# Retention loads issued by SP, the first pair's ahead of the stage; first keys turned on GpSimd; the rotation split around the head factor

## What is computed

```python
def retention_mixer(p, positions):
    q, k, v, g = _split(p, RET_SIZES)
    q = rotary(q, positions); k = rotary(k, positions) * (dk ** -0.5)
    def step(R, inp):                      # one chunk of 128 tokens
        s = einsum('bihd,bjhd->bhij', qc, kc) * decay_mask
        inner = einsum('bhij,bjhe->bihe', s, vc)
        cross = einsum('bihd,bhde->bihe', qc * q_decay, R)
        R = R * chunk_decay + einsum('bjhd,bjhe->bhde', kc * k_decay, vc)
        return R, inner + cross
    o = group_norm_heads(o, RET_GN_EPS)
    return silu(g) * o
merged = sigmoid(g_rw) * (y_rw @ w_branch_rw) + sigmoid(g_ret) * (y_ret @ w_branch_ret)
```

## Time and profile before

| what | value |
|---|---|
| median of three runs | 2634.45 us (2625.81 to 2635.38) |
| the profiled execution | 2635.51 us, its span 2633.5 us |
| PE busy over the span | 2428.1 us, 92% |
| DVE busy | 1237.1 us, 47% |
| ACT busy | 672.1 us, 26% |
| POOL busy | 752.0 us, 29% |
| chain that ended last, by engine | PE 77%, DVE 12%, DVEq 4%, ACT 3%, DMA 2% |

### The profile page before, as it was taken

How to read it: one execution, slowest core, us unless ns; L and a number is a source line. 1 busy time by engine, 2 the same in 40 slices (tenths; PEclk the granted TensorE clock), 3 DMA queues, 4 the chain that set the end, 5 groups by cost and what they waited for, 6 DMA issues and landing times.

```text
span 2633.5 us, 33584 instructions
## 1 busy us (share of the span) xinstructions
PE 2428.1 (92%) x12944; PEld 1961.6 (74%) x12944; DVE 1237.1 (47%) x1382; ACT 672.1 (26%) x1020; POOL 752.0 (29%) x386
## 2 busy tenths in 40 slices
PE   5899989999998996888998999999999986989896
PEld 4788878877886885777787788888777864767674
DVE  6644264335335442756556644444411417526623
ACT  3322222122222221333242211111223332023421
POOL 2311221131123110113464333333244434222132
PEclk9999999999999998999998999999999997999997
DMA  3211111121111115634443111111142220111011
GB/s 121 64 49 49 65 48 57 49 71 51 49 65 56 49 49 153 203 122 172 159 147 109 56 48 42 46 48 48 41 151 95 93 75 24 43 56 41 17 40 64
DMA packets 54872, 196.46 MB, mean 75 GB/s; under 512 B 5744, under 2 KB 7152, under 8 KB 53872
## 3 DMA queue, kind: packets, MB, share of 16 engines
q1 hardware_dynamic: 29952, 109.07, 12.6%
q10 hardware_dynamic: 24816, 85.84, 9.2%
HBM read 158.71 MB, written 36.18 MB: 74 GB/s over the span
## 4 chain that ended last, share of the span: by engine, by line
PE 77%; DVE 12%; DVEq 4%; ACT 3%; DMA 2%; issue 2%; ACTq 1%; POOL 0%; POOLq 0%; SPq 0%
PE psg L336 10%; PE psg L341 10%; PE psg L340 10%; PE psg L471 5%; PE psg L473 5%; PE psg L466 5%; PE psg L851 1%; PE psg L855 1%; PE psg L854 1%; PE psa L562 1%; PE psg L912 1%; PE psg L907 1%; PE psb L551 1%; PE psg L914 1%; PE psg L365 1%
## 5 line engine op out<-in xcount | busy, mean ns | idle before, releaser
L286 POOL CAST whi<-wraw 128x1024 fp32r<-128x1024 f32 (+1 forms) x164 | 186.9, 1139 | 1637.1 <-PE psg L466 612.3
L336 PE MATMUL psg<-xhi,whi 128*128 128x512 f32 x1152 | 459.7, 399 | 3.1 <-DVE pu L1461 2.7
L341 PE MATMUL psg<-xhi,wlo 128*128 128x512 f32 x1152 | 454.6, 395 | 0.0
L340 PE MATMUL psg<-xlo,whi 128*128 128x512 f32 x1152 | 452.9, 393 | 0.0
L288 POOL TENSOR_TENSOR wlo<-wraw,whi 128x1024 fp32r<-128x1024 f32 (+1 forms) x164 | 432.0, 2634 | 25.7 <-issue 6.3
L473 PE MATMUL psg<-xhi,wlo 128*128 128x512 f32 x640 | 260.8, 408 | 0.0
L466 PE MATMUL psg<-xhi,whi 128*128 128x512 f32 x640 | 260.0, 406 | 0.0
L471 PE MATMUL psg<-xlo,whi 128*128 128x512 f32 x640 | 259.9, 406 | 0.0
L336 PEld LDWEIGHTS psg<-xhi,whi 128*128 128x128 f32 x1152 | 216.3, 188 | 56.5 <-issue 5.1
L341 PEld LDWEIGHTS psg<-xhi,wlo 128*128 128x128 f32 x1152 | 216.2, 188 | 54.5
L340 PEld LDWEIGHTS psg<-xlo,whi 128*128 128x128 f32 x1152 | 216.2, 188 | 52.7 <-issue 1.0
(11 more groups left out here) (469 smaller groups left out, 4464.4 us busy)
## 6 DMA issues: line engine op xcount, KB each, us to landing
wraw<-w SPq DMA_DIRECT2D x208, 512.0 KB, 3.4
later_scratch<-stage ACTq DMA_DIRECT2D x40, 512.0 KB, 2.7
xres<-xt ACTq DMA_DIRECT2D x4, 1024.0 KB, 11.4
RV<-later_scratch ACTq DMA_DIRECT2D x4, 1024.0 KB, 12.2
RG<-later_scratch ACTq DMA_DIRECT2D x4, 1024.0 KB, 7.4
later_scratch<-rstage ACTq DMA_DIRECT2D x8, 512.0 KB, 2.7
mgr<-later_scratch ACTq DMA_DIRECT2D x8, 512.0 KB, 3.6
mgt<-later_scratch ACTq DMA_DIRECT2D x8, 512.0 KB, 4.6
```

The lines of the kernel that those rows point to most:

```text
L286: pool.tensor_copy(whi[:, u, 0:width], wraw[:, u, 0:width])
L336: mm = pe.matmul(psg[b][:, cols], whi[:, slot, w_cols], rhs_hi(k, cols), start=(k == 0), stop=False)
L340: pe.matmul(psg[b][:, cols], whi[:, slot, w_cols], rhs_lo(k, cols), start=False, stop=False)
L341: mm = pe.matmul(psg[b][:, cols], wlo[:, slot, w_cols], rhs_hi(k, cols), start=False, stop=(k == kts - 1))
```

## The change

- SP issues all retention loads, in between its weight blocks. The first pair's and the angles wait on tr_act 32 (ACT has copied the values of the last recurrent group), three of the RWKV results on gh_ready 16 in the same group. The fourth stays where it was made. The first pair gets tiles of its own (rraw_first, rswp_first, RTAB_first, RG0, RQD0, RKD0).
- The first pair's keys are turned and scaled by GpSimd, in four instructions behind the split of block 57 (B_BRW - 1). DVE turns only that pair's queries.
- For the other pairs `rotate` falls into two parts: the products stand where it stood, the sum and the keys' scaling between the two head factors.
- The first pair's second values go to psg[1] instead of psb, so that they need not wait for ACT's copy of the first.
- For p > 0 six of the branch matmuls move from behind the scores to ahead of the chunk sums.
- At the end the first two tiles of yret are split while the last head factor is under way, and PE does their product (12 matmuls) ahead of the last L410.

```diff
...
-        RV, RG = tiles("RV", 12, [P, 2, T]), tiles("RG", 14, [P, 2, T])
+        yrw = [tiles("yrw0", 9, [P, T]), tiles("yrw1", 2, [P, T]), tiles("yrw2", 3, [P, T]), YB]
+        RV, RG = tiles("RV", 12, [P, 2, T]), [spare("RG0", 0, [P, 2, T]), tiles("RG", 14, [P, 2, T])]
+        RQD = [tiles("RQD0", 6, [P, T]), tiles("RQD", 16, [P, T])]
+        RKD = [tiles("RKD0", 7, [P, T]), tiles("RKD", 17, [P, T])]
...
-        rraw = [spare("rraw0", 0, [P, 2, T]), tiles("rraw1", 18, [P, 2, T])]
-        rswp = spare("rswp", 2, [P, 2, T])
+        rraw = [tiles("rraw_first", 4, [P, 2, T]), tiles("rraw1", 18, [P, 2, T]), spare("rraw0", 0, [P, 2, T])]
+        rraw.append(rraw[1])
+        rswp = [tiles("rswp_first", 6, [P, 2, T]), spare("rswp", 2, [P, 2, T])]
...
+            def load_pair(p):
+                sp.dma_start(RTAB[p], ret_tab[p]).then_inc(sem("ret_in"), 16)
+                rows = later_d[6 * p:6 * p + 2]
+                sp.dma_start(rraw[p][:, :, :], rows.rearrange("a p t -> p a t")).then_inc(sem("ret_in"), 16)
+                for q in range(4):
+                    dst, src = q * 32, (q ^ 1) * 32
+                    sp.dma_start(rswp[1][dst:dst + 32, :, :], rows[:, src:src + 32, :].rearrange("a p t -> p a t")
+                                 ).then_inc(sem("ret_in"), 16)
+                load_values(p)
...
+            stream(0, B_BRW, 0)
+            for b in range(2):
+                sp.wait_ge(sem(f"stored{b}"), 80 + 16)
+            sp.wait_ge(sem("rot_stored"), 64)
+            sp.wait_ge(sem("tr_act"), 8 * PAIRS)
+            sp.dma_start(RTAB[0][:, :, :], ret_tab[0]).then_inc(sem("ret_in"), 16)
+            first_rows(1, sem("ret_in"))
+            for r in range(4):
+                sp.dma_start(rott[r * 32:r * 32 + 32, :, :], rot_d[:, 2 * (r % 2):2 * (r % 2) + 2, :]
+                             ).then_inc(sem("rot_in"), 16)
+            sp.dma_start(RC[:, :], mats[:, M_CENT_RET, :]).then_inc(sem("rv_in"), 16)
+            load_values(0)
+            first_rows(0, sem("rq_in"))
+            sp.wait_ge(sem("yrw_stored"), 16 * PAIRS)
+            sp.wait_ge(sem("gh_ready"), GROUPS * PAIRS)
+            for r in range(PAIRS - 1):
+                sp.dma_start(yrw[r][:, :], yrw_d[:, r, :]).then_inc(sem("yrw_in"), 16)
+            stream(B_BRW, B_BRW + 2, 0)
+            sp.wait_ge(g_full, T_BRW)
+            load_gates(0)
+            sp.wait_ge(sem("yrw_done"), PAIRS)
+            sp.wait_ge(sem("rv_tr"), 2)
+            for b in range(2):
+                sp.wait_ge(sem(f"stored{b}"), 80 * (PAIRS - 1) + 16)
+            load_pair(1)
+            for p in range(1, PAIRS):
+                stream(B_BRW + 2 * p, B_BRW + 2 * p + 2, 0)
+                sp.wait_ge(sem("rg_done"), p)
+                load_gates(p)
+                if p + 1 < PAIRS:
+                    sp.wait_ge(sem("rkd"), p + 1)
+                    sp.wait_ge(sem("rs_ready"), 2 * p)
+                    sp.wait_ge(sem("rv_tr"), 2 * p + 2)
+                    load_pair(p + 1)
+            stream(B_MRG, B_OUT + KT, 0)
...
             split_blocks(0, B_BRW)
+            pool.wait_ge(sem("ret_in"), 96)
+            pool.wait_ge(sem("rot_in"), 64)
+            key, other = rraw[0][:, 1, :], rswp[0][:, 1, :]
+            pool.tensor_tensor(key, key, rott[:, 1, :], ALU.mult)
+            pool.tensor_tensor(other, other, rott[:, 0, :], ALU.mult)
+            pool.drain()
+            pool.tensor_tensor(key, key, other, ALU.add)
+            pool.drain()
+            pool.tensor_tensor(RKD[0][:, :].rearrange("p (n c) -> p n c", c=P), key.rearrange("p (n c) -> p n c", c=P),
+                               RTAB[0][:, 3:4, :].broadcast_to([P, NB, P]), ALU.mult).then_inc(sem("rkd"), 1)
             split_blocks(B_BRW, B_MRG, PAIRS * P)
...
+                    if between and k == 2:
+                        between()
...
-                if h == 0:
+                dst = psb_t
+                if p == 0 and h == 1:
+                    pe.wait_ge(g_free[1], 8 * PAIRS + 2)
+                    dst = psc_t
+                elif h == 0:
...
-                pe.wait_ge(sem("rv_tm"), 2 * p + 2)
+                pe.wait_ge(sem("rv_tm"), 2 * p + 2 if p else 1)
...
-                q_k = rraw[p % 2]
+                q_k = rraw[p]
+                if p:
+                    fill_branch(6)
                 pe.wait_ge(sem("rk_tm"), p + 1)
+                pe.wait_ge(sem("rv_tm"), 2 * p + 2)
...
-                fill_branch(12)
+                fill_branch(6 if p else 12)
...
-                ret_spread(p, 1)
                 if p + 1 < PAIRS:
+                    ret_spread(p, 1)
...
+            streamed(B_MRG, T_MRG, sem("op_split"), SPLIT_BEFORE["yret"], between=lambda: ret_spread(PAIRS - 1, 1))
...
+            def rotate_products(p):
+
+                v.wait_ge(sem("ret_in"), 96 * p + 96)
+                tt(rraw[p][:, :, :], rraw[p][:, :, :], turned(p, 1), MUL)
+                tt(rswp[1][:, :, :], rswp[1][:, :, :], turned(p, 0), MUL)
+
+            def rotate_sum(p):
+
+                v.drain()
+                tt(rraw[p][:, :, :], rraw[p][:, :, :], rswp[1][:, :, :], ADD)
+                v.drain()
+                tt(by_token(RKD[1]), rraw[p][:, 1, :].rearrange("p (n c) -> p n c", c=P),
+                   RTAB[p][:, 3:4, :].broadcast_to([P, NB, P]), MUL).then_inc(sem("rkd"), 1)
...
             v.memset(id2[:, :], 1.0)
-            rotate(0)
-            v.wait_ge(sem("yrw_stored"), 16 * PAIRS + 16)
+            v.wait_ge(sem("rot_in"), 64)
+            v.wait_ge(sem("ret_in"), 96)
+            v.wait_ge(sem("rq_in"), 80)
+            query, other = rraw[0][:, 0, :], rswp[0][:, 0, :]
+            tt(query, query, rott[:, 1, :], MUL)
+            tt(other, other, rott[:, 0, :], MUL)
+            v.drain()
+            tt(query, query, other, ADD)
+            v.drain()
             decay_queries(0)
-            split_low("yrw", yrw, xhi, xlo, PAIRS)
+            for j in range(PAIRS):
+                operand_low("yrw", yrw[j][:, :], j)
+            for b in range(2):
+                v.wait_ge(sem(f"stored{b}"), 80 * PAIRS + 16)
...
-                    rotate(p + 1)
+                    rotate_products(p + 1)
...
+                    if h == 0 and p + 1 < PAIRS:
+                        rotate_sum(p + 1)
+                    elif h == 0:
+                        for j in range(2):
+                            operand_low("yret", yret[:, j, :], j)
+                if p == 0:
+                    v.wait_ge(sem("yrw_stored"), 16 * PAIRS + 16)
                 if p + 1 < PAIRS:
                     decay_queries(p + 1)
-            split_low("yret", yret, xhi, xlo, KT)
+            for j in range(2, KT):
+                operand_low("yret", yret[:, j, :], j)
...
-            load_values(0)
...
-            load_queries_keys(0)
-            s.wait_ge(sem("yrw_stored"), 16 * PAIRS + 16)
-            s.dma_start(yrw[:, :, :], yrw_d).then_inc(sem("yrw_in"), 16)
-            for b in range(2):
-                s.wait_ge(sem(f"stored{b}"), 80 * PAIRS + 16)
-            load_gates(0)
+            def operand_high(src, j):
+                act(xhi[:, j, :], src, CP).then_inc(sem("op_high"), 1)
+
             for h in range(2):
                 values(0, h)
             keys(0)
-            s.wait_ge(sem("yrw_in"), 16)
-            high("yrw", yrw, xhi, PAIRS)
...
-                    s.wait_ge(sem("rkd") if p else sem("rqd"), p + 1)
-                    load_queries_keys(p + 1)
-                    load_values(p + 1)
...
                     values(p + 1, 0)
+                else:
+                    s.sem_inc(g_free[0], PAIRS)
+                    operand_high(yret[:, 0, :], 0)
+                    operand_high(yret[:, 1, :], 1)
...
-            for b in range(2):
-                s.sem_inc(g_free[b], PAIRS)
+            s.wait_ge(sem("yret_done"), KT - 1)
+            for j in range(2, KT - 1):
+                operand_high(yret[:, j, :], j)
             s.wait_ge(sem("yret_done"), KT)
-            high("yret", yret, xhi, KT)
+            s.sem_inc(g_free[1], PAIRS)
+            operand_high(yret[:, KT - 1, :], KT - 1)```

`first_rows(part, landed)` issues the rows of one part of pair 0 (1 keys, 0 queries) into rraw_first and their exchanged halves into rswp_first: five DMAs each.

**GpSimd at the end of the recurrent stage.** Before, the loop over blocks of 1024 columns is followed at once by that over blocks of 512:

```order
L286 CAST whi<-wraw 128x1024 [waits w_used]
L288 TENSOR_TENSOR wlo<-wraw,whi 128x1024
L292 REGISTER_ALU
L292 COMPARE_AND_BRANCH
L292 UNCONDITIONAL_BRANCH
L292 ISA
L284 ISA [waits w_landed0]
L286 CAST whi<-wraw 128x512 [waits w_used]
```

More of the change, by code:

```diff
@@ L267, in stream, with first_rows @@
                                      ).then_inc(w_landed[u], 16)
-            stream(0, B_OUT + KT, 0)
+            def first_rows(part, landed):
+                rows = later_d[part:part + 1]
```

(30 more changed lines are left out.)

70 lines of the change are left out of this document (29 added, 41 removed).

## The result

The changed kernel takes 2592.46 us (median of four runs, 2590.74 to 2597.12) where the kernel before takes 2630.13 (four runs, 2625.14 to 2635.38): a ratio of 0.986, 95% interval 0.9847 to 0.9874, or 37.7 us. The forecast was 2599, the range 2590 to 2610. The profiled execution took 2592.28 us, its span 2590.5, against 2635.51 and 2633.5 before.

The account below looks back on a forecast made before the run. PE was taken to be held by waits around retention: late loads, head factors, key copies. Entry 23.1, pairs 8.6, six matmuls 1.1 and end 2 sum to 34.8 us off 2635.51, 2600.7; as a median, forecast 2599 us, range 2590 to 2610.

Parts of the forecast that it names:

- The entry (A): Entry into retention: early loads and keys on GpSimd start the first branch matmul at about 1037, not 1060.18; 23.1 us.
- The pairs (B): Between pairs: less rotation ahead of the first head factor and earlier loads shorten PE's waits and half clock; 8.6 us.
- C: Pairs 1 to 3: six matmuls cover ACT's key copy, less a new 0.7 us wait; 1.1 us, bounds 0 and 3.3.
- the 0.5 that I had kept as a bound: Pairs: extra gain in each if less work ahead of the head factor also shortens pair 0's 1.12 us wait.
- The fit of the second part: Between the two head factors: the rest of `rotate`, about 3.6 us, fits DVE's 3.94 us idle time, 0.3 to spare.
- The end (D): End of retention: twelve matmuls ahead of the last transpose win 3.8 us, less clock fall and collision; 2 us.
- The collision that I had priced: At the end: GpSimd's split meets DVE's copy RE<-sm; by the ports rule the 3.8 us shrink by about 1.4.
- half clock at the entry: Rival: PE stays at half clock at the entry, which gives 16.6 us; 2606 us; chance 0.15, shared with a missed fit.
- the small steps of the recurrent group: Rival: GpSimd's four key instructions hold up DVE's small steps from 994 to 1004, losing 9.6 us; 2609 us; chance 0.03.
- weight block late for PE: Rival: weight blocks queue behind a pair's loads on SP and PE stands in each pair's first fill; slower, chance 0.02.
- the one that says how late: Rival: first loads come only with block 58's split, at 1012, so the entry gives 16 us; 2607 us; chance 0.05.

Follow-up runs that it names:

- The late loads: The changed kernel, with the first pair's loads issued only when the fourth RWKV result is done; median 2610.87 us, ratio 0.9916 to the kernel before.
- the keys on DVE: The changed kernel, with the first pair's keys turned and scaled by DVE ahead of its queries instead of by GpSimd; median 2593.69 us, ratio 0.9849.
- the repeat of the change: The changed kernel run once more, unaltered, beside the kernels with a reworked end; median 2591.47 us, ratio 0.9853 to the kernel before.
- ninth experiment: The new end, plus ACT squaring both heads before copying the branch product, and five and seven branch matmuls instead of six and six; median 2580.95 us.
- the new end: The changed kernel, with four yret tiles split earlier in pair 3, two more around the last transpose, and own tiles for that; median 2585.30 us.

## Why the prediction was right

- **The entry (A), forecast 23.1, measured 23.5.** Each step stood: loads from 975, keys at 1000.6, which is 1004.2 on the old axis, since this execution was 3.6 us ahead there (forecast 1004), GpSimd's multiply at the price of its subtract (2.40), PE at full clock, 11.9 us to the first branch matmul (forecast 12). The late loads show that none of it is there without the head start, and the keys on DVE that GpSimd's share of it is 4.75 us. The prediction said that the list of waits names three causes; it has a fourth, the 7.9 us for the turned keys shown above. They are part of the same entry, so no term was missing. The second values in psg[1] have no experiment of their own; PE's one wait of 1.1 us between the two halves is gone.
- **The pairs (B), forecast 8.6, measured 10.5** (the pairs without C's 1.1). The mechanism was right, one term was short: "What is late next is ACT ... That is pair 0's 1.12 us, and it stays". It did not stay but fell to 0.52 to 0.56 in each of three pairs, the 0.5 that I had kept as a bound. Rows of the kernel before that I had not read show what it held: in pair 0 GpSimd's subtract ran into the copy that the factor waits for. In the changed kernel that copy begins 0.1 to 0.2 us behind the subtract, in each of pairs 0 to 2. GpSimd and DVE in pair 0, before:

```profile
1076.45 1.28 POOL L288 TENSOR_TENSOR wlo<-wraw,whi 128x512 fp32r<-128x512 f32 x1
...
1077.01 1.26 DVE L1246 COPY RE<-sm 128x1024 f32<-128x1024 f32 x1
```

and after:

```profile
1048.47 1.30 POOL L353 TENSOR_TENSOR wlo<-wraw,whi 128x512 fp32r<-128x512 f32 x1
...
1049.88 0.69 DVE L1339 COPY RE<-sm 128x1024 f32<-128x1024 f32 x1
```

- **One sum for two cures.** I had also given the split and the earlier load one sum, as though both were needed; either brings most of it.
- **The fit of the second part** with 0.3 us to spare was right to a tenth: DVE's idle time ahead of the second factor is 0.26.
- **Six matmuls ahead (C), forecast 1.1, measured 1.1**, with the new wait of 0.7 at 0.58, 0.57 and 0.57.
- **The end (D), forecast 2, measured 0.0 and -2.3.** Here the step that failed is the twelve matmuls, "2.8 us, ahead of the transpose, once ACT and DVE have split the first tile (about 1.6 us)". ACT copied the branch tile first, so PE waited 2.28, and then it was at half clock: 0.63 us for a matmul, spaced 0.43 and not 0.23, 4.24 us for the twelve. From the last sums to the third tile it was 12.9 us before, 9.5 by the forecast's terms (a gain of 3.4, not the 3.8 it states) and 11.3 measured. The 1.6 us won were lost again behind the wait of 3.75 (forecast 4.0), where twelve matmuls took 4.45 us and not 2.80. In the repeat of the change the two twelves took 5.25 and 5.28. I had counted the clock's fall once, and not behind the first wait. The collision that I had priced hardly came: the copy began ahead of the subtract, in the last 0.4 us of GpSimd's cast, and took 0.90.
- **The Trainium skill**, "SBUF — State Buffer", section "Who interferes with whom", says that whichever of DVE (in a two-port mode) and GpSimd issues first has the shared ports for its whole instruction and the other is blocked, and that a DVE instruction with two SBUF inputs contends with GpSimd too. These traces agree. The copy took 1.26 us in pair 0 before and 1.89 us in pair 3 after, when the subtract had begun first, and 0.69 when the copy had (ninth experiment); DVE's product with two inputs in SBUF took 3.36 us beside GpSimd instead of 1.22 (first).
- **The rivals.** None was seen: no half clock at the entry, loads from 975, the small steps of the recurrent group at their old length, and no weight block late for PE, though GpSimd waited 7.70 us for one. The rivals priced late loads at a gain of 16 to 16.6 us of the 23.1; the one that says how late has them start at 1012. Loads that go out only after the last RWKV result leave nothing of the gain (-0.4).

The sum was 34.8 us and the three stages give 35.1; that they agree so well is luck, since B's excess and D's shortfall cancel. The 37.7 us between medians, and the 43.2 between the profiled executions, hold 2.6 and 8 us more that these stages do not. The result lies 6.5 us under the forecast: 2.2 of it because 37.7 us were saved where the forecast, counted from 2634.45, saves 35.5, and 4.3 because the kernel before, with its fourth run, has a median of 2630.13.

## What to carry to other kernels

Where a stage opens with loads that wait for the last result of the stage before, find which of them do not need that result: a head start, with the keys turned by GpSimd in the same gap, was worth 23.5 us of 37.7 here, and 4.75 of them were the arithmetic that the idle engine took over. Before splitting work around a critical step, ask whether an earlier load already removes the wait. At the end of a stage, put matmuls ahead of a wait only if their operands are ready by then: the same twelve matmuls ahead of the last transpose gave nothing with two tiles split on the spot, and the end gained 8.2 us with four tiles split earlier in the last pair and two more around the transpose.

## What the runs showed of the hardware

- In the changed kernel GpSimd's multiply and add of 128x1024 float32 tiles in SBUF cost 2.39 to 2.40 us, as its subtract does; DVE takes 1.22 to 1.23.
- Of a DVE copy and a GpSimd subtract, who begins first decides who pays: in the ninth experiment the copy began 0.04 us ahead of GpSimd's subtract and kept its 0.69 us, and the subtract took 2.90 instead of 2.36; the other way round, in the changed kernel, the copy took 1.89.
- The same code takes times that differ by several us between executions: up to the end of the recurrent stage, the twelve other profiled executions lie from 1.1 us later to 7.8 us earlier than that of before, and two executions of one kernel (the new end) differ by 7.8 us behind retention. Gains of 1 to 5 us could be read only by setting the same matmuls of two traces against each other within the changed stage.
